# State-space input products over a 96-row stack, laid out by on-chip copies, and a load ring of six slots

## The reference, cut to what matters

```python
proj = xn @ w_in
q, k, v, u_ssm, h_conv, b_gate, c_gate, gate_logits = jnp.split(proj, IN_SPLITS, axis=-1)
...
# inside s5_ssm: u is 256 wide, 16 groups of 16 inputs, 64 states each
bu_re = jnp.einsum('gph,blgh->blgp', bb_re, ug)
bu_im = jnp.einsum('gph,blgh->blgp', bb_im, ug)
...
_, _, s_re, s_im = lax.associative_scan(combine, (a_re, a_im, bu_re, bu_im), axis=1)
...
merged = g[:, :, 0] * y_a + g[:, :, 1] * y_b + g[:, :, 2] * y_c
return merged @ w_out
```

## Time and profile before

| what | value |
|---|---|
| median of 3 runs | 1540.18 us (1537.77 to 1540.42) |
| the profiled execution, whole time | 1538.63 us |
| its span, first to last instruction | 1536.9 us |
| mean granted TensorE clock | 0.994 |
| layer 0's mixer, from start to its last wo product | about 0 to 234 us |
| layer 1's mixer | about 480 to 690 us |
| the experts | 699 to 1532 us |

### The profile page before, as it was taken

One profiled execution on the slowest core, in us unless ns is written; L12 is line 12 of the kernel. 1 busy time (PEld: TensorE's weight loads), 2 busy tenths in 40 slices (PEclk: granted clock), 3 DMA queues, 4 the chain that ended last, 5 costly groups with the idle time before them and its releaser, 6 DMA issues.

```text
span 1536.9 us, 30324 instructions
## 1 busy us (share of the span) xinstructions
PE 1502.9 (98%) x13463; PEld 922.1 (60%) x13463; DVE 599.6 (39%) x925; ACT 347.7 (23%) x427; POOL 219.5 (14%) x283
## 2 busy tenths in 40 slices
PE   7999999999999999999999999999999999999997
PEld 6988999999999988994333333333333323333331
DVE  6888667755556477564111211211202012011021
ACT  5443355444445453331000000000000000000001
POOL 3447369300000137200000000000000000000000
PEclk9999999999999999999999999999999999999998
DMA  9732395554554522589999999999999999999995
GB/s 275 234 110 83 116 282 166 191 192 165 192 192 151 174 88 83 165 325 385 372 392 419 419 419 419 419 419 420 419 419 420 420 418 419 419 419 420 419 419 222
DMA packets 146339, 465.00 MB, mean 303 GB/s; under 512 B 10144, under 2 KB 92064, under 8 KB 131872
## 3 DMA queue, kind: packets, MB, share of 16 engines
q1 hardware_dynamic: 143296, 461.40, 77.7%
q0 software_dynamic: 416, 1.05, 0.3%
q10 hardware_dynamic: 2496, 0.61, 0.3%
HBM read 461.98 MB, written 1.05 MB: 301 GB/s over the span
## 4 chain that ended last, share of the span: by engine, by line
PE 59%; DMA 5%; SPq 3%; ACT 1%; DVE 1%; issue 0%; POOL 0%; DVEq 0%; ACTq 0%; POOLq 0%
PE work L1141 14%; PE acc L1159 13%; PE work L752 11%; PE acc L1141 11%; PE ssm_y L1141 4%; SPq L647 3%; DMA moe_ring<-in_moe_w_down 2%; DMA moe_ring<-in_moe_w_gate 2%; DMA moe_ring<-in_moe_w_up 2%; PE acc L1096 1%; PE acc L1109 1%; PE work L873 0%; PE acc L752 0%; PE acc L843 0%; PE work L779 0%
## 5 line engine op out<-in xcount | busy, mean ns | idle before, releaser
L752 PE MATMUL work<-xs,parts 128*128 128x256 f32 x3600 | 455.3, 287 | 9.7 <-DVE xs L1508 4.8
L752 PEld LDWEIGHTS work<-xs,parts 128*128 128x128 f32 x3600 | 442.2, 193 | 19.7 <-issue 15.7
L1141 PE MATMUL work<-moe_ring,arena 128*32 128x448 f32 x2688 | 276.1, 539 | 0.1
L1501 DVE TENSOR_TENSOR parts<-ring,parts 128x2048 fp32r<-128x2048 f32 x94 | 220.0, 2345 | 121.8 <-ACT parts L1235 121.7
L1159 PE MATMUL acc<-moe_ring,arena 128*32 128x512 f32 x2352 | 257.6, 593 | 8.6 <-DMA moe_ring<-in_moe_w_down 7.0
L1141 PE MATMUL acc<-moe_ring,arena 128*32 128x448 f32 x2048 | 216.5, 540 | 1.0 <-ACT arena L1421 0.8
L1235 ACT ACTIVATE parts<-ring 128x2048 fp32r<-128x2048 f32 x94 | 178.7, 1907 | 89.3 <-PE work L752 62.6
L1159 PEld LDWEIGHTS acc<-moe_ring,arena 128*32 128x32 f32 x2352 | 75.8, 110 | 186.2 <-issue 167.9
L1141 PEld LDWEIGHTS work<-moe_ring,arena 128*32 128x32 f32 x2688 | 87.3, 110 | 165.7 <-issue 160.7
L1908 DVE TENSOR_TENSOR arena<-arena,work 128x448 f32<-128x448 f32 x42 | 23.7, 616 | 347.9 <-ACT arena L1421 347.9
L1421 ACT ACTIVATE arena<-acc 128x448 f32<-128x448 f32 x32 | 15.7, 541 | 633.5 <-PE work L1141 633.5
(11 more groups left out here) (312 smaller groups left out, 1060.3 us busy)
## 6 DMA issues: line engine op xcount, KB each, us to landing
moe_ring<-in_moe_w_gate SPq DMA_DIRECT2D x128, 896.0 KB, 23.8
moe_ring<-in_moe_w_up SPq DMA_DIRECT2D x128, 896.0 KB, 23.7
moe_ring<-in_moe_w_down SPq DMA_DIRECT2D x112, 1024.0 KB, 25.2
ring<-in_w_in SPq DMA_DIRECT2D x44, 1024.0 KB, 6.5
ring<-in_dense_w_gate SPq DMA_DIRECT2D x14, 1024.0 KB, 5.3
ring<-in_dense_w_up SPq DMA_DIRECT2D x14, 1024.0 KB, 5.1
ring<-in_dense_w_down SPq DMA_DIRECT2D x14, 1024.0 KB, 4.9
ring<-in_w_out SPq DMA_DIRECT2D x8, 1024.0 KB, 13.0
```

Of the source, the lines that this page charges most:

```text
L752: last = nc.tensor.matmul(out_ap, a, b, start=start and n == 0, stop=stop and n == len(pairs) - 1, skip_group_check=shared)
L1141: last = nc.tensor.matmul(banks[g][GRP * q:GRP * q + GRP, 0:CHUNK], x, w[:, q * CHUNK:q * CHUNK + CHUNK], start=k == 0, stop=k == KT - 1, ...
L1501: tt(parts[:, s % PARTS, 1, :], ring[:, n % RING, :], parts[:, s % PARTS, 0, :].bitcast(F32), ALU.subtract).then_inc(lo_ready, 1)
```

## The change

The product bu becomes one fp32r matmul over 96 rows: the rows of B high, B high and B low stand under each other, against u high, u low and u high. `b_stack` (96 rows, 8 steps, real and imaginary part, 128) takes one slot of 1 MB, so the ring has six instead of seven; `u_stack` takes the place of `hs`. ACT writes the high parts (`b_high` at bbT, `u_high` at u), DVE the low parts. SP then moves 32 rows at a time into the stacks, twelve DMAs of 64 KB for B and twelve for u in each layer, between its loads: those of B before the load of unit 13 (gC3), those of u before that of unit 15 (brA0). `b_high` and `b_low` stand where `hconv` and `bconv` do, so ACT's copies of h and b wait until B is stacked; `u_low` stands in `sig`, so ACT's first sigmoid waits until u is stacked. The first turn of the experts' loads is put in an order computed from what lies under each of them. The rest is unchanged.

```diff
-    RING = 7
+    RING = 6
...
+            b_stack = before_experts.enter_context(nc.sbuf_tensor("b_stack", [P, SJ, 2, P], F32R))
...
-        bbT = sb("bbT", [P, 4, P])
+        u_high = sb("u_high", [P, CT * L])
...
+        b_high, b_low = flat_conv
+        u_low = sig[:, :, :].rearrange("p t n -> p (t n)")
...
-                    "bbT": (bbT_ready, l + 1), "u": (u_ready, l + 1), "h": (h_conv_ready, l + 1),
+                    "bbT": (b_low_ready, l + 1), "u": (u_ready, l + 1), "h": (h_conv_ready, l + 1),
...
+        STACKED = 16 * STACK * (P // 32)
...
+            def stack_b(l):
+                sp.wait_ge(b_low_ready, l + 1)
+                for block, part in enumerate((b_high, b_high, b_low)):
+                    for m in range(P // 32):
+                        to = b_stack[rows_of(block), :, :, :].rearrange("r (a m) c n -> r m a (c n)", m=P // 32)
+                        sp.dma_start(to[:, m, :, :].bitcast(F32),
+                                     part[rows_of(m), :].rearrange("r (a n) -> r a n", n=2 * P)).then_inc(b_stacked, 16)
+
+            def stack_u(l):
+                sp.wait_ge(u_low_ready, l + 1)
+                for block, part in enumerate((u_high, u_low, u_high)):
...
             for n, (l, name) in enumerate(STREAM):
                 if n == 1:
                     sp.wait_ge(params_loaded, 16 * PARAMS)
+                if n - RING == STREAM.index((l, "u0")) + 1:
+                    stack_b(l)
+                if n - RING == STREAM.index((l, "u0")) + 3:
+                    stack_u(l)
...
+            for s in sorted(range(FIRST_TURN), key=lambda s: (free_after(s)[-1][0], s)):
+                for _, signal, value in free_after(s):
+                    sp.wait_ge(signal, value)
                 load_unit(*UNITS[s], 0, True)
...
                         if t == 0:
-                            pe.wait_ge(bbT_ready, l + 1)
-                            pe.wait_ge(u_ready, l + 1)
-                        a, b = t // 4, 32 * (t % 4)
+                            pe.wait_ge(b_stacked, STACKED * (l + 1))
+                            pe.wait_ge(u_stacked, STACKED * (l + 1))
                         for q in range(2):
-                            last = nc.tensor.matmul(bank[:, q * L:q * L + L], bbT[b:b + 32, 2 * q + a, :],
-                                                    uT[b:b + 32, a, :], start=True, stop=True)
+                            last = nc.tensor.matmul(bank[:, q * L:q * L + L], b_stack[0:32 * STACK, t, q, :],
+                                                    u_stack[0:32 * STACK, t, :], start=True, stop=True)
...
                     elif kind in ("h", "b"):
                         bank = arrived(Group((l, kind, t)))
+                        act.wait_ge(b_stacked, STACKED * (l + 1))
...
-                        nc.scalar.activation(bbT[:, :, :].rearrange("p t n -> p (t n)"), bank[:, :], ACT.Copy)\
-                            .then_inc(bbT_ready, 1)
+                        nc.scalar.activation(b_high.bitcast(F32R), bank[:, :], ACT.Copy).then_inc(b_high_ready, 1)
+                    elif kind == "u":
+                        bank = arrived(Group((l, kind, t)))
+                        nc.scalar.activation(u_high[:, :].bitcast(F32R), bank[:, :], ACT.Copy).then_inc(u_high_ready, 1)
...
+                        if kind == "gC" and t == 0:
+                            act.wait_ge(u_stacked, STACKED * (l + 1))
...
                     elif kind == "u":
                         bank = arrived(Group((l, kind, t)))
+                        dve.wait_ge(u_high_ready, l + 1)
+                        tt(u_low.bitcast(F32R), bank[:, :], u_high[:, :], ALU.subtract).then_inc(u_low_ready, 1)
...
+                    elif kind == "bbT":
+                        bank = arrived(Group((l, kind, t)))
+                        dve.wait_ge(b_high_ready, l + 1)
+                        tt(b_low.bitcast(F32R), bank[:, :], b_high, ALU.subtract).then_inc(b_low_ready, 1)
```

More of the change, by code:

```diff
@@ L118, in uses_in @@
         return HALF_UNITS // 2 if kind == "gu" else D_UNITS
-    RING = 7
+    RING = 6
     PARTS = 3
+    STACK = 3
     BR_AT = RING * UW
-    PARTS_AT = BR_AT + UW
+    BB_AT = BR_AT + UW
+    PARTS_AT = BB_AT + UW
     HS_AT = PARTS_AT + 2 * PARTS * UW
@@ L327, in trunk_kernel @@
         x_parts = [xs[:, q * KT * L:(q + 1) * KT * L].rearrange("p (k n) -> p k n", n=L) for q in range(2)]
+        u_stack = hs[:, :].rearrange("p (t n) -> p t n", n=L)
         h_parts = hs[:, :].rearrange("p (b q f n) -> p b q f n", b=2, q=2, n=L)
@@ L386, in trunk_kernel @@
         v_tiles = v[:, :, :].rearrange("p t n -> p (t n)").rearrange("p (t n) -> p t n", n=L)
+        flat_conv = [conv[:, :, :].rearrange("p t n -> p (t n)") for conv in (hconv, bconv)]
+        b_high, b_low = flat_conv
+        u_low = sig[:, :, :].rearrange("p t n -> p (t n)")
         scaled_pair = attn[:, :, :].rearrange("p h n -> p (h n)")[:, 0:4 * L].rearrange("p (b q n) -> p b q n", b=2, q=2)
@@ L444, in trunk_kernel @@
         bbp_ready = sem("bbp_ready")
-        bbT_ready = sem("bbT_ready")
+        b_high_ready = sem("b_high_ready")
+        b_low_ready = sem("b_low_ready")
+        b_stacked = sem("b_stacked")
+        u_high_ready = sem("u_high_ready")
+        u_low_ready = sem("u_low_ready")
+        u_stacked = sem("u_stacked")
         start_ready = sem("start_ready")
@@ L606, in _, with rows_of @@
                     .then_inc(x_loaded[half], 16)
+            def rows_of(m):
+                return slice(32 * m, 32 * m + 32)
+            def stack_b(l):
[8 more added lines that the diff above has]
+                for block, part in enumerate((u_high, u_low, u_high)):
+                    for m in range(P // 32):
+                        to = u_stack[rows_of(block), :, :].rearrange("r (a m) n -> r m a n", m=P // 32)
+                        sp.dma_start(to[:, m, :, :].bitcast(F32),
+                                     part[rows_of(m), :].rearrange("r (a n) -> r a n", n=L)).then_inc(u_stacked, 16)
             for n, (l, name) in enumerate(STREAM):
@@ L657, in load_block, with free_after @@
                 return waited
-            def under(s):
+            def free_after(s):
                 lo, hi = PLACE[UNITS[s]]
[L661 to L665, removed]
-                load_unit(*UNITS[s], 0, True)
-            def last_part_under(s):
-                slots = [(at - PARTS_AT // UW) // 2 for at in under(s) if PARTS_AT // UW <= at < HS_AT // UW]
-                return max((n for n in range(S0 - PARTS, S0) if n % PARTS in slots), default=-1)
@@ L672, in _ @@
[L672 to L689, removed]
+                def meets(start, size):
+                    return lo < start + size and start < hi
@@ new lines, in free_after @@
+                after = []
+                for j in range(RING):
+                    if meets((len(STREAM) - RING + j) % RING * UW, UW):
+                        split_no = S0 - RING + j
+                        after.append((split_no - PARTS + 0.8, lo_ready, split_no + 1))
+                if meets(BR_AT, UW):
+                    after.append((S0 - 5 + 0.1, work_done, Group((DEPTH - 1, "gB", KT - 1)).done))
+                if meets(BB_AT, UW) or meets(HS_AT, XS_AT - HS_AT):
+                    after.append((0, work_done, Group((DEPTH - 1, "bu", SJ - 1)).done))
@@ new lines, in free_after @@
+                for part in range(S0 - PARTS, S0):
+                    if meets(PARTS_AT + part % PARTS * 2 * UW, 2 * UW):
+                        after.append((part + 0.1, *used_up(*SPLIT[part])))
+                if meets(XS_AT, MOE_SIZE - XS_AT):
+                    after.append((S0 - 1 + 0.1, *used_up(*SPLIT[S0 - 1])))
+                return sorted(after, key=lambda entry: entry[0])
+            for s in sorted(range(FIRST_TURN), key=lambda s: (free_after(s)[-1][0], s)):
+                for _, signal, value in free_after(s):
+                    sp.wait_ge(signal, value)
+                load_unit(*UNITS[s], 0, True)
@@ L864, in _ @@
                             last = nc.tensor.transpose(bank[:, q * P:q * P + P],
-                                                       bbp[:, q // 2, (q % 2) * P:(q % 2) * P + P], ident[:, :])
+                                                       bbp[:, q % 2, (q // 2) * P:(q // 2) * P + P], ident[:, :])
                         last.then_inc(work_done, 1)
```

## The result

| | before | after |
|---|---|---|
| median | 1539.97 us (1537.77 to 1540.42, 4 runs) | 1567.03 us (1564.01 to 1568.04, 4 runs) |
| ratio, with 95% interval | 1 | 1.0175 (1.0162 to 1.0187) |
| profiled execution, its span | 1538.63 us, 1536.9 us | 1564.01 us, 1562.3 us |
| mean granted TensorE clock | 0.994 | 0.987 |

Between the two profiled executions it is 25.4 us, where the sum had 17.1.

What follows compares the result with a forecast made beforehand. TensorE, busy 1502.9 of 1536.9 us, was taken as the bound; 1538.63 - 13.0 (product) + 0.7 (B's low part) + 23.8 (wait before glu) + 5.6 (clock) gave 1556 us, range 1546 to 1568.

Steps and rivals of the forecast that it cites:

- the sum: Whole kernel: profiled 1538.63 us, less 13.0, plus 0.7, 23.8 and 5.6, gives 1555.7 us.
- The stall: Before glu, gB1's late load holds up the gelu: TensorE stands still 11.9 us a layer, 23.8 in all.
- T + 11.7: In each mixer, the gelu ends 11.7 us after T, the end of gA 7.
- The product: In the mixers' bu steps, the new product costs 0.24 us instead of 1.25, saving 1.0 each.
- The rival of 0.65: At each bu, the tile switch cost stays: 0.65 us a product, 5.7 us less gained, 1561 us; chance 0.12.
- The gain of the product: Over both mixers, seven of eight bu a layer count, 14.0 us, less 0.5 a layer for DVE: 13.0.
- The other side: Before glu, gB1 isn't late, so the product's gain stands alone: 1526 us; chance 0.06.
- The copies: Stacking B and u in each layer: twelve copies take 6.2 us, are hidden, and cost nothing.
- ahead of gC0 by about as much: In layer 0, B's copies run from 69.8 to 76 us, hidden by about layer 1's margin, 8 us and more.
- The clock: Behind the wait before glu, TensorE's lowered clock loses 2.8 us a layer (bounds 1.5 and 3.5), 5.6 in all.
- Nothing else: Dense part, first phase and experts lose nothing from six slots or the new load order.
- The low part of B: In layer 0 on DVE, it stands ahead of the split of b0 that TensorE awaits: 0.7 us lost.

Runs made afterwards that it cites:

- e1: Changed kernel with brA0 and brA1 one unit later in the load stream, so gB1 takes gA1's slot; 1540.44 us, ratio 1.0012 to the kernel before.
- e3: Kernel before with only the six-slot ring and the new order of experts' loads, old product, no copies; 1571.09 us, ratio 1.0204.
- e2: e1 with B's high and low parts moved to free tiles of merged, so the copy of h waits for no stack; 1536.46 us, ratio 0.9984.
- e4: Changed kernel with 45 constant products on TensorE ahead of its wait for the gelu; 1559.29 us, ratio 1.0129 to the kernel before.
- e11: Kernel before, with only bu 6 and 7 behind gates 9 and 10 instead of 10 and 11; 1538.71 us, ratio 1.0003.
- e10: e2 with bu 6 and 7 behind gates 9 and 10 instead of 10 and 11; 1532.63 us, ratio 0.9960 to the kernel before.

## Why the prediction was right and wrong

**The stall: right.** T + 11.7 was worked out for glu against the end of gA 7; it came at T + 11.99 (176.22 to 188.21), in each layer, with the row at the split of gB1, the issue at gA 7's end and the order of the rows behind it as told (12.02 of idle time in layer 1). e1 takes it away with one unit's place in the stream, e3 has it without any copy. The load landed some 5.36 us after its issue, where 5.28 was taken.

**The product: right.** 0.25 us a bu behind a gA step, 0.24 forecast; no switch of tile shows. The rival of 0.65 falls, and with it its time of 1561 us, though that lies nearer to the result than the forecast does. I had laid its price to what the Trainium skill says, "TensorEngine Tiling (Array Packing)", section Key Properties, of a change of mode that drains TensorE. For 32 rows the trace agrees that there is a price: from gA's branch product to the next row it is 1.82 us ahead of the old bu (148.62 to 150.44) and 1.54 ahead of a product over 128 rows (160.33 to 161.87). Ahead of the new bu it is 1.54 as well (153.95 to 155.49): 96 rows between 128 leave no room for a drain. The price of the 32 rows was read a little low: 24 fp32r passes take 3.06 us of the step and not 2.9, which makes it 0.48 and the rival 0.72.

**The gain of the product: mechanism right, size wrong.** 6.5 us a layer were forecast, 5.2 came in each. Tail 1 waits 1.41 and 1.31 us, 1.3 forecast. For DVE falling behind I took 0.5 a layer; layer 1 has 0.84 at ys 0 and 0.47 at ys 1, 1.3 in all. And two of the bu in each layer, the one behind attention and the one behind ys 0, saved 0.8 and not 1.0 (556.26 to 560.29 before, 571.02 to 574.24 after). I named DVE as the next engine from its busy share, and did not follow the chain through POOL to ys 1, which had 2.2 us to spare. In the kernel after, the fault of the ring hid most of this: the late load of gB1 kept the split of the gB units away from POOL's chain. With the loads in time, as in e1 (the split at 623.48, and beside it an operation of POOL of 2.77 us), POOL's part in layer 1 took 8.9 us instead of 6.7, and the wait at ys 1 grew from 0.47 us to 2.5 and 2.8, and the gain nearly vanished. The other side among my rivals (gB1 isn't late: 1526) was thus also priced wrong: e1 and e2 are that case, with 1540 and 1536.

**The copies, "Cost: nothing": wrong, the step that failed.** Three things in it. The issue was taken from the four output stores at 0.34 us; these copies take 0.60, so that twelve last 9.7 us, not 6.2. In layer 0 "ahead of gC0 by about as much" looked at when TensorE needs the split of gC0, and not at what stands behind this split on DVE: a second split and the convolution, which before ended at 90.31, only 1.9 us ahead of the branch product at 92.17. And the wait of ACT's copy of h was followed through in layer 1 alone, where it cost nothing in the runs either. Measured in layer 0: a wait of 3.04 us and 1.4 of half clock, 4.8 in all with the slower steps between. e2 recovers 4.0 us by moving one buffer.

**The clock: right in kind, its size in part luck.** 2.8 a layer forecast, 1.7 and 2.9 measured, and e4's comparison gives 1.6 and 2.9. The forecast rested on one row, the 14.44 us behind the wait of 2.69. That row differs between executions of the same instructions: e11 is the kernel before up to there, and took 11.75 us for the 96 matmuls; e1 is the kernel after up to there, and took 14.42 where that took 13.18. Over all thirteen profiled executions it was 11.75 (twice), 13.2 (eight times) or 14.2 to 14.4 (three times), behind waits of 2.7 to 3.4 us. In e11:

```profile
71.89 11.75 PE L752 MATMUL work<-xs,parts 128*128 128x256 f32 x96 [2.73 <-DVE parts L1501]
```

So what a wait costs by the clock is to be forecast as a range, for a wait of some 3 us here from nothing to 2.7 us. The granted clock over 9 us behind the wait in layer 1 (us, busy of PE, PEld, DVE, ACT, POOL, PEclk, DMA share, GB/s):

```profile
656.00:665.00 9.00, 8.54 (x38) 7.76 (x39) 3.83 (x4) 4.38 (x5) 0.00 (x0) 0.64 1.10 349
```

Of these 9 us, 6.5 are at 1.2 GHz instead of 2.4 if the rest are at full clock. In e4, where TensorE was busy up to 2 us before glu, no matmul behind it is slow.

**"Nothing else": wrong by 2.9 us.** The experts are neutral, as forecast (25.7 us late at their start, 25.4 at the end). But layer 0's last steps and its dense part cost 2.9 us more. A wait of TensorE for DVE has 1.33 us there where none was. e3 has 1.31 in the same place, e1 none, so it comes with the ring's fault and not with the copies. It stands at 252.99, behind five operations of DVE: two on `xs` and three on `rstd`, which take 1.46 and 2.46 us, before 1.00 and 1.51. Beside them POOL has operations of 128x256 for layer 1's parameters. e3 has the same rows (1.45 and 2.45); in e4, as late, POOL has only operations of 128x8 and 128x128 there, DVE takes 1.22 and 1.74, and the wait is absent. So these rows speak for POOL's slowing DVE, but no run was made to tell it apart, and its cause stays open. Of the rest of the 2.9 us, 0.5 is a wait for DVE at 289.38 that was not there before, and 0.3 a longer one at the start of the dense part.

**The other numbers.** The low part of B cost 0.6 us (TensorE's wait for that split is 3.32 us instead of 2.69), 0.7 forecast; that the 96 matmuls behind it took 13.18 us instead of 14.44 is no work of the change but the spread of the clock told above. The sum missed by 8.3 us against the profiled execution: copies 4.8, product 2.6, dense part 2.9, stall 0.5, less 1.0 for the clock, 1.3 up to gC 0 and 0.3 at the end.

## What to carry to other kernels

When a buffer ring loses a slot, write down for each late unit which older unit's slot it takes and what frees that one; a unit that follows a long-held one by exactly the ring's length is where it breaks, and one exchange in the stream may be the cure. A wait is to be priced by what stands behind it on its engine in program order up to the next hand-over to the bottleneck, not by the first thing that needs it. And when the bottleneck engine gets faster, look for every chain that has been finishing just ahead of it: here a gain of 5.7 us met 2.2 us of slack, and 3.1 were left; and a change of order that was worth nothing before was worth 3.8 us after.

## What the runs showed of the hardware

- A small copy within the chip costs SP 0.60 us of issue (585 to 1568 ns, 24 of them), against 0.34 for an output store, and lands 2.0 us later (median; the slowest 3.0), or 5.2 (median) for those of u, which follow two 1 MB loads.
- A POOL operation on 128x256 elements takes 0.73 us alone and 2.6 to 2.8 when it begins shortly after a DVE split of 128x2048, which is about the split's own length. The view of the first of POOL's six operations in e2 (min, median, max) shows that this is the common case:

```profile
L2132 POOL TENSOR_TENSOR arena<-arena x16: 730/2633/2779, 102.3 to 616.0; 128x256 f32<-128x256 f32 x16
```

The Trainium skill, "SBUF — State Buffer", section "SBUF: two separate sides", says that GpSimd and a VectorE operation with two inputs in SBUF share one pair of ports, taken whole for an instruction, so that the other blocks. The split has two such inputs, and the 2.63 us agree: the operation waits the split out. In e10 the chain ends before the last split begins, and the second long operation of bu 7's chain (2.77 us in e2) is a short one again.
- Behind a wait of 2.7 to 3.4 us of TensorE, the same 96 matmuls took 11.75, 13.2 or 14.4 us, in different executions of the same instructions.
- Two matmuls over 96 rows stand between matmuls over 128 rows at no cost that these rows show (0.25 us for the pair), while four over 32 rows in fp32 cost 1.25.
